# Turning the first unit of a feed-forward network in 32x32 blocks on VectorE, moving the blocks by DMA, and running that unit second

## The chip, the cores and the metric

The kernel runs on one core of a Trainium2 chip. The metric is the device time of one execution in microseconds (us): 575.26 us is the median of three runs of the kernel before (575.2 to 575.7). A lower time is better.

## What is computed

A decoder trunk of two layers over 256 tokens of 1024 features, all in float32: layer 0 mixes tokens with a gated short convolution, layer 1 with causal attention over eight heads that reads K and V projected once after layer 0. Each layer ends in the same feed-forward network, and the change is about the beginning of that network:

```python
def conv_ffn(h, w_up, w_conv, b_conv, w_down):     # h: 256 x 1024, F = 2816
    g, u = jnp.split(h @ w_up, 2, axis=-1)
    g = causal_dwconv(g, w_conv) + b_conv          # three taps along the tokens
    return (jax.nn.silu(g) * u) @ w_down

x = x + conv_ffn(rmsnorm(x, norm_ffn[i]), ffn_w_up[i], ffn_conv[i], ffn_conv_b[i], ffn_w_down[i])
```

## The kernel before, in words

**Weights.** All weights are cut into 106 slots of 128 x 2048 float32 (1 MB). SyncE (SP) loads them in order into a ring of six raw buffers (`load`, line 341); the load of slot s waits until slot s-6 has been split. ScalarE (ACT) writes the high part of a slot (`hi`, line 427), VectorE (DVE) the rest (`lo`, line 775), and TensorE (PE) multiplies high by high, high by low and low by high. Each engine works through a queue of its own, in the order in which the code is written, and the engines wait for each other on semaphores (`slot_done`, `f_cross`, `f_sum`, `tap0`, `conv_op`, `silu_done`, `act_full`, `act_hi_ready`, `act_lo_ready` and others).

**A network.** There are 22 pairs of 128 gate and up features, in 11 units of 256 features: a gate slot, an up slot and, for the unit two places earlier, a down slot. F stands below for the first slot of a network (`FFN[l]`, l = 0 and 1), so F and F+1 are gate and up of unit 0, F+2 and F+3 those of unit 1, F+4 and F+5 those of unit 2, F+6 is the down slot of unit 0, F+7 and F+8 are gate and up of unit 3, F+9 is the down slot of unit 1, and so on. From unit 1 on, a slot (`wide_slot`, `project`, lines 1215 and 1223) leaves features on partitions and tokens along the row in PSUM bank pair 0 (gate) or 1 (up). ACT copies the cross terms out (line 537 or 544), DVE adds the main term (914, 918), ACT applies the first tap and the bias (`tap_zero`, 515), DVE the two other taps (`taps`, 893), ACT the silu (523), DVE multiplies by the up half (`glued`, 900), ACT writes the high part of the product (`acts`, 527) and DVE the low part (905). `down` (lines 1278 to 1282) multiplies the product by the down slot. A bank pair is free for the next unit when DVE has read it (`f_sum`).

**The opening.** Unit 0 comes right behind the norm, when the normed activations become ready 128 tokens at a time. `open_two` (`rows_of_two`, lines 1265 and 1270) therefore makes it with tokens on partitions: tokens 0 to 127 into bank `by_rows[0]` (it signals `rows_done`), tokens 128 to 255 into `by_rows[1]` (`slot_done`), each 128 x 512. ACT copies each of them to SBUF (`copy_opening`, 509), and TensorE transposes each with four 128x128 transposes into banks `acc00` and `acc01` (`turn_opening`, 1359): the four for the first tokens stand ahead of slot F+2, the four for the others between its two halves (`two_after_opening`). Unit 0 then goes through taps, silu, product and split on ACT and DVE ahead of unit 1. The order on PE behind the opening is: slot F+2, F+3, F+4, F+5, down slot F+6 (`down(l, 2)`, waits for the low part of unit 0's product), F+7, F+8, F+9, and so on. The order of ACT and DVE is that of `ffn(l)` in their blocks. Both networks are built by the same functions.

Of the kernel before, what the change touches and what calls it, by code (L numbers as in the profile page):

```python
# [28 lines left out]
P = 128  # L29
EPS = 1e-6  # L30
RAW = 6
# [29 lines left out]
def build(nc, x, x_columns, weights, params, norm_ffn, final_norm, out, F, TAPS):  # L61
# [52 lines left out]
    assert place(V0 - 2) == place(V0 + 2) == place(V0 + 6) and place(V0 - 1) == place(V0 + 3) == place(V0 + 5)  # L114

    def gate_slot(l, j):
        return FFN[l] + (2 * j if j < 2 else 3 * j - 2)
# [8 lines left out]
    with ExitStack() as ctx:  # L126
        def sb(name, shape, dt=F32):
            return ctx.enter_context(nc.sbuf_tensor(name, shape, dt))
# [23 lines left out]
        ident = sb("ident", [P, P])  # L152
        warm_tile = sb("warm_tile", [P, P])
        par = sb("par", [P, TAPS * KD + 2 * ((TAPS + 1) * FT + KD)])
        inv_ms = sb("inv_ms", [P, 2])
# [20 lines left out]
        logits = scratch[:, 0:768].rearrange("p (e n) -> p e n", e=2)  # L176
        opening = scratch[:, 1024:2048].rearrange("p (t n) -> p t n", t=2)
        whole = scratch[:, 1024:2048].rearrange("p (b e n) -> p b e n", b=2, e=2)
# [41 lines left out]
        late_normed = sem("late_normed")  # L220
        opening_copied = sem("opening_copied")
        opening_T = sem("opening_T")
        first_landed = [sem(f"first_landed{q}") for q in range(3)]
# [110 lines left out]
        def _(sp):  # L334
# [34 lines left out]
            load_half(3, 0, fourth_landed)  # L369
            load_half(3, 1, landed[3])  # L370
            for s in range(4, SLOTS):
                load(s)
            for h in range(2):
# [47 lines left out]
        def _(act):  # L421
# [80 lines left out]

            def copy_opening(s, t, o, r):

                if t:
                    act.wait_ge(slot_done, s + 2)
                else:
                    act.wait_ge(rows_done, r)
                act.activation(opening[:, t, :], by_rows[t], ACT.Copy).then_inc(opening_copied, 1)

            def tap_zero(l, j, gate, turn=None):
# [17 lines left out]
            def unit(l, j, turn=None):  # L529

                s, U = gate_slot(l, j), l * UNITS + j
                if j >= 3:
                    hi(s + 2, turn)
                act.wait_ge(slot_done, after(s + 1, turn, TURN))
                if U:
                    act.wait_ge(conv_op, after(4 * U, turn, 4 * LOOPED))
                act.activation(whole[:, 0], cross[0], ACT.Copy).then_inc(f_cross, 1)  # L537
                hi(s + 3, turn)
                act.wait_ge(f_sum, after(f_turn(l, j, 0), turn, 2 * LOOPED))
                tap_zero(l, j, whole[:, 0], turn)  # L540
                silu(U, j, turn)
                act.wait_ge(slot_done, after(s + 2, turn, TURN))
                act.wait_ge(act_full, after(U, turn, LOOPED))
                act.activation(whole[:, 1], cross[1], ACT.Copy).then_inc(f_cross, 1)  # L544
                hi(s + 4, turn)
                acts(U, j, turn)

            def ffn(l):
                s, U = FFN[l], l * UNITS
                copy_opening(s, 0, l, 1 if l == 0 else 4)  # L550
                hi(s + 3)
                copy_opening(s, 1, l, None)
                hi(s + 4)
                act.wait_ge(opening_T, 2 * l + 1)
                tap_zero(l, 0, acc[0][0][:].rearrange("p (e n) -> p e n", e=2))
                silu(U, 0)
                acts(U, 0)
                unit(l, 1)
                unit(l, 2)
                with act.Fori(0, TURNS) as turn:  # L560
                    for j in range(3, 3 + LOOPED):
                        unit(l, j, turn)
                if l == 0:
                    hi_ahead(1)
                    hi(V0)
# [204 lines left out]
        def _(dve):  # L770
# [113 lines left out]
            def taps(l, j, gate, turn=None):  # L884
                U, g = l * UNITS + j, glu[:, j % 2]
                dve.wait_ge(tap0, after(U + 1, turn, LOOPED))
                for back in (1, 2):
                    for e in range(2):
                        if back == 2:
                            dve.wait_ge(conv_op, after(4 * U + e + 1, turn, 4 * LOOPED))  # L890
                        f = after(2 * j + e, turn, 2 * LOOPED)
                        dst = g[:, e, back:S]
                        dve.scalar_tensor_tensor(out=dst, in0=gate[:, e, 0:S - back],  # L893
                                                 scalar=f_par[:, l, bass.ds(f + (TAPS - 1 - back) * FT, 1)],
                                                 in1=dst, op0=ALU.mult, op1=ALU.add).then_inc(conv_op, 1)

            def glued(l, j, up, turn=None):
                U, g = l * UNITS + j, glu[:, j % 2]
                dve.wait_ge(silu_done, after(U + 1, turn, LOOPED))
                dve.tensor_tensor(g, g, up, ALU.mult).then_inc(act_full, 1)  # L900

            def acts(l, j, turn=None):
                U, g = l * UNITS + j, glu[:, j % 2]
                dve.wait_ge(act_hi_ready, after(U + 1, turn, LOOPED))
# [3 lines left out]
            def unit(l, j, turn=None):  # L908
# [13 lines left out]
                acts(l, j, turn)  # L922

            def ffn(l):
                s = FFN[l]
                lo(s + 2)
                lo(s + 3)
                lo(s + 4)
                taps(l, 0, acc[0][0][:].rearrange("p (e n) -> p e n", e=2))
                dve.wait_ge(opening_T, 2 * l + 2)  # L930
                glued(l, 0, acc[0][1][:].rearrange("p (e n) -> p e n", e=2))
                acts(l, 0)
                unit(l, 1)
                unit(l, 2)
                with dve.Fori(0, TURNS) as turn:
# [248 lines left out]
        def _(pe):  # L1184
# [168 lines left out]

            def turn_opening(o, t):

                pe.wait_ge(opening_copied, 2 * o + t + 1)
                for b in range(2):
                    for e in range(2):
                        last = pe.transpose(acc[0][b][:, 256 * e + P * t:256 * e + P * t + P],
                                            opening[:, t, 256 * b + P * e:256 * b + P * e + P], ident[:])  # L1360
                    if t:
                        last.then_inc(opening_T, 1)

            def two_after_opening(s, o):

                wait_slot(s)
                turn_opening(o, 0)
                project(s, 0, hA, (0,))
                turn_opening(o, 1)
                project(s, 0, hA, (1,)).then_inc(slot_done, 1)  # L1370
                wide_slot(s + 1, 1, hA)

# [26 lines left out]
            def down(l, j, turn=None):  # L1399

                U = l * UNITS + j - 2
                pe.wait_ge(act_lo_ready, after(U + 1, turn, LOOPED))
# [210 lines left out]
```

## Time and profile before

| | |
|---|---|
| median of 3 runs | 575.26 us |
| the profiled execution | 575.42 us |
| its span, from the first to the last instruction | 573.6 us |
| granted TensorE clock, mean share of full speed | 0.998 |
| busy: PE, weight loads of PE, DVE, ACT, POOL | 99%, 85%, 73%, 56%, 4% |
| DMA: share of the span on 16 engines | 52% |

The views used below are: the page's busy shares; the waits of one engine (what it sat idle for, in total, how often, longest); the chain of work that ended last, in order of time; the timeline of one engine (start, duration, line, operation, count, and in brackets the idle time before it); the groups of instructions by line and shape; and the list of DMA issues with the time to landing. In the chain a matmul counts from the end of the one before it to its own end; in the timeline it counts from its own start, and as matmuls are pipelined one of 512 columns lasts 0.39 us there while the next starts 0.23 us behind it.

### The profile page before, as it was taken

The page shows a single profiled execution, that of the slowest core. Times are in us where ns is not written, and L with a number is a line of the kernel's source. Part 1 is how long each engine was busy: PE and PEld are TensorE (multiplying, and loading weights), DVE is VectorE, ACT ScalarE, POOL GpSimd, SP SyncE. Part 2 cuts the span into 40 slices and gives each one's busy share as a digit, 9 for nine tenths or more (in the row PEclk, how much of TensorE's full clock was granted, in tenths as well). Part 3 has the DMA queues.
Part 4 walks back from the last instruction along what each step waited for, and adds up shares of the span by engine and source line. Part 5 has one row for each costly group of instructions (what it writes and reads, how often), then busy time and mean ns, then how long its engine had stood idle before and what let it go on. Part 6 is the DMA issues. An engine that isn't in the chain of part 4 may idle for free.

```text
span 573.6 us, 7862 instructions
## 1 busy us (share of the span) xinstructions
PE 566.0 (99%) x3036; PEld 489.7 (85%) x3036; DVE 418.2 (73%) x514; ACT 321.8 (56%) x415; POOL 21.6 (4%) x26
## 2 busy tenths in 40 slices
PE   8999999999999999999999999999999999999996
PEld 7888988898888888888888899888988888888885
DVE  4799987678666666676886688896786666666764
ACT  6844554565655455457456766745656554554543
POOL 0114001000000000000000000210000000000001
PEclk9999999999999999999999999999999999999999
DMA  8986656446555556555544443364355555564001
GB/s 281 419 334 231 237 193 256 184 146 212 178 198 221 180 187 219 163 191 164 216 163 177 175 149 146 117 250 185 147 202 183 201 221 175 192 220 147 1 2 73
DMA packets 17314, 108.08 MB, mean 188 GB/s; under 512 B 1920, under 2 KB 2176, under 8 KB 5248
## 3 DMA queue, kind: packets, MB, share of 16 engines
q1 hardware_dynamic: 16128, 104.78, 50.0%
q10 hardware_dynamic: 1152, 2.82, 1.4%
q8 instruction: 24, 0.39, 0.3%
q14 instruction: 10, 0.08, 0.0%
HBM read 106.55 MB, written 1.05 MB: 188 GB/s over the span
## 4 chain that ended last, share of the span: by engine, by line
PE 94%; DVE 2%; DMA 1%; issue 1%; POOL 0%; ACT 0%; SPq 0%; POOLq 0%; DVEq 0%
PE pair L1215 35%; PE pair L1223 18%; PE acc L1278 8%; PE acc L1280 8%; PE acc L1282 8%; PE pair L1265 5%; PE pair L1270 3%; PE pair L1240 1%; DMA raw<-in_weights 1%; PE acc L1190 1%; PE acc L1189 1%; PE acc L1188 1%; PE pair L1292 1%; PE pair L1249 1%; DVE wgt L775 1%
## 5 line engine op out<-in xcount | busy, mean ns | idle before, releaser
L775 DVE TENSOR_TENSOR wgt<-raw,wgt 128x2048 fp32r<-128x2048 f32 x90 | 206.2, 2297 | 56.6 <-ACT wgt L427 56.3
L1215 PE MATMUL pair<-hA,wgt 128*128 128x512 f32 x832 | 197.9, 391 | 0.0
L427 ACT ACTIVATE wgt<-raw 128x2048 fp32r<-128x2048 f32 x91 | 173.7, 1911 | 22.3 <-PE acc L1282 21.7
L1215 PEld LDWEIGHTS pair<-hA,wgt 128*128 128x128 f32 x832 | 154.1, 188 | 30.7
L1223 PEld LDWEIGHTS pair<-hA,wgt 128*128 128x128 f32 x832 | 103.8, 191 | 3.0 <-DVE gain L944 0.6
L1223 PE MATMUL pair<-hA,wgt 128*128 128x256 f32 x832 | 104.8, 283 | 0.4 <-DVE gain L944 0.4
L1278 PE MATMUL acc<-wgt,kq_hi 128*128 128x512 f32 x156 | 48.0, 389 | 0.0
L1282 PE MATMUL acc<-wgt,kq_lo 128*128 128x512 f32 x156 | 48.0, 389 | 0.0
L1280 PE MATMUL acc<-wgt,kq_hi 128*128 128x512 f32 x156 | 48.0, 389 | 0.0
L523 ACT ACTIVATE begin<-begin 128x512 f32<-128x512 f32 x22 | 13.9, 633 | 59.7 <-DVE begin L893 59.7
L537 ACT ACTIVATE begin<-pair 128x512 f32<-128x512 f32 x20 | 11.9, 594 | 58.3 <-PE pair L1223 58.3
L914 DVE TENSOR_TENSOR begin<-begin,pair 128x512 f32<-128x512 f32 x20 | 13.7, 686 | 30.9 <-ACT begin L537 30.9
L1278 PEld LDWEIGHTS acc<-wgt,kq_hi 128*128 128x128 f32 x156 | 29.3, 188 | 6.1
L1280 PEld LDWEIGHTS acc<-wgt,kq_hi 128*128 128x128 f32 x156 | 29.3, 188 | 6.1
L1282 PEld LDWEIGHTS acc<-wgt,kq_lo 128*128 128x128 f32 x156 | 29.3, 188 | 6.1
L893 DVE SCALAR_TENSOR_TENSOR begin<-begin,par 128x255 f32<-128x255 f32 (+1 forms) x80 | 33.2, 477 | 0.0
L1265 PE MATMUL pair<-wgt,hA 128*128 128x512 f32 x128 | 32.6, 393 | 0.0
L918 DVE TENSOR_TENSOR begin<-begin,pair 128x512 f32<-128x512 f32 x20 | 13.8, 688 | 23.7 <-ACT begin L544 23.7
L1265 PEld LDWEIGHTS pair<-wgt,hA 128*128 128x128 f32 x128 | 23.7, 188 | 5.1 <-issue 0.3
L386 POOL TENSOR_TENSOR rstd<-msq,minus_half 128x1 f32<-128x1 f32 x10 | 7.6, 758 | 421.1 <-DVE msq L807 417.4
L515 ACT ACTIVATE begin<-begin,par 128x256 f32<-128x256 f32 x40 | 21.6, 589 | 1.5 <-DVE begin L914 1.5
L444 ACT ACTIVATE acc<-xs 128x512 f32<-128x512 f32 x19 | 11.3, 597 | 19.8 <-DVE xs L796 15.4
(181 smaller groups left out, 614.5 us busy)
## 6 DMA issues: line engine op xcount, KB each, us to landing
raw<-in_weights SPq DMA_DIRECT2D x94, 1024.0 KB, 4.8
raw<-in_weights SPq DMA_DIRECT2D x8, 256.0 KB, 8.4
raw<-in_weights SPq DMA_DIRECT2D x4, 512.0 KB, 11.0
xs<-in_x SPq DMA_DIRECT2D x2, 512.0 KB, 10.3
gain<-in_norm_ffn ACTq DMA_DIRECT2D x2, 512.0 KB, 3.6
begin<-in_x_columns ACTq DMA_DIRECT2D x3, 256.0 KB, 7.7
gain<-in_final_norm ACTq DMA_DIRECT2D x1, 512.0 KB, 5.2
out<-begin SPq DMA_DIRECT2D x2, 256.0 KB, 2.0
```

The costliest lines, as they stand in the source:

```text
L427: act.activation(split_slot(s)[0], raw[:, s % RAW, :], ACT.Copy).then_inc(w_hi_ready, 2 if s + 1 in AHEAD else 1)
L515: ins = act.activation(g[:, e, :], gate[:, e, :], ACT.Identity, bias=f_par[:, l, bass.ds(f + TAPS * FT, 1)], scale=f_par[:, l, bass.ds(f + ...
L523: act.activation(g, g, ACT.Silu).then_inc(silu_done, 1)
L775: dve.tensor_tensor(wlo, raw[:, s % RAW, :], whi.bitcast(F32), ALU.subtract).then_inc(w_lo_ready, 2 if s + 1 in AHEAD else 1)
L893: dve.scalar_tensor_tensor(out=dst, in0=gate[:, e, 0:S - back], scalar=f_par[:, l, bass.ds(f + (TAPS - 1 - back) * FT, 1)], in1=dst, op0=A ...
L1215: last = pe.matmul(pair[b][:, e, :].rearrange("p (a n) -> p a n", a=2), whi[:, w], hid[:, :, k, :], start=first and k == 0, stop=not first ...
L1223: last = pe.matmul(pair[b][:, e, 0:S], wlo[:, w], hid[:, 0, k, :], start=first and k == 0, stop=k == KD - 1)
L1265: pe.matmul(dst, hA[:, 0, k, tok], wgt[:, part, a:b + 1:b - a, w], start=k == 0 and part == 0, stop=False)
L1270: last = pe.matmul(dst, hA[:, 1, k, tok], wgt[:, 0, a:b + 1:b - a, w], start=False, stop=k == KD - 1)
L1278: pe.matmul(acc[t][h][:], ah, wh[h], start=first, stop=False)
L1280: pe.matmul(acc[t][h][:], ah, wl[h], start=False, stop=False)
L1282: last = pe.matmul(acc[t][h][:], al, wh[h], start=False, stop=h == closes)
```

## The change

- The eight transposes of each opening on TensorE and ACT's two copies to SBUF are gone. In their place DVE transposes each `by_rows` bank from PSUM to SBUF in one instruction of 32x32 blocks (`turn_opening` on DVE; it writes into `v_own`, which is idle then), and SP issues 16 DMAs for each 128 tokens (`move_opening`) that carry pieces of 32 partitions x 512 bytes from `v_own` to `kq_first` (also idle then). The 16 DMAs for tokens 0 to 127 stand ahead of the load of slot F+8 in SP's queue, those for tokens 128 to 255 ahead of that of F+9.
- PE runs slots F+2 and F+3 as ordinary slots, each behind a wait for one of the two VectorE transposes (they read the banks that the slots overwrite).
- On ACT and DVE unit 1 now comes first and unit 0 second (`opened_unit`), then unit 2. The semaphore counts follow (`unit_count`). PE's order of slots is as before.
- In `opened_unit` ACT first waits for the 32 DMAs and copies the gate half into `v_own` (two copies of 128 x 256), applies the first tap from there, and DVE makes the product in two halves of 128 x 256.
- ACT's table load for silu is called forth by a tiny silu of 2 columns ahead of unit 1.

```diff
--- before.py
+++ after.py
@@ -112,6 +112,10 @@
 
     assert place(V0 + 4) == place(V0) == 2
     assert place(V0 - 2) == place(V0 + 2) == place(V0 + 6) and place(V0 - 1) == place(V0 + 3) == place(V0 + 5)
+
+    def unit_count(l, j):
+
+        return l * UNITS + (1 - j if j < 2 else j)
 
     def gate_slot(l, j):
         return FFN[l] + (2 * j if j < 2 else 3 * j - 2)
@@ -151,6 +155,7 @@
         dist = sb("dist", [P, 384])
         ident = sb("ident", [P, P])
         warm_tile = sb("warm_tile", [P, P])
+        silu_warm = sb("silu_warm", [P, 2])
         par = sb("par", [P, TAPS * KD + 2 * ((TAPS + 1) * FT + KD)])
         inv_ms = sb("inv_ms", [P, 2])
         sumsq = sb("sumsq", [P, 2, 2])
@@ -174,7 +179,9 @@
         conv_out = scratch.rearrange("p (f n) -> p f n", f=KD)
         glu = scratch[:, 0:1024].rearrange("p (b e n) -> p b e n", b=2, e=2)
         logits = scratch[:, 0:768].rearrange("p (e n) -> p e n", e=2)
-        opening = scratch[:, 1024:2048].rearrange("p (t n) -> p t n", t=2)
+        open_blocks = v_own[:].rearrange("p (t m n) -> p t m n", t=2, m=4)
+        opened = kq_first[:].rearrange("p a b c n -> p (a b c n)").rearrange("p (t g e n) -> p (t g) e n", t=2, g=4, e=4)
+        open_gate = v_own[:, 0:512].rearrange("p (e n) -> p e n", e=2)
         whole = scratch[:, 1024:2048].rearrange("p (b e n) -> p b e n", b=2, e=2)
         a_whole = gain[:].rearrange("p (b e n) -> p b e n", b=2, e=2)
         act_hi = kq_hi[:].rearrange("p a b n -> p (a b n)").rearrange("p (u e n) -> p u e n", u=4, e=2)
@@ -218,8 +225,10 @@
         x_T = sem("x_T")
         kv_scaled = sem("kv_scaled")
         late_normed = sem("late_normed")
-        opening_copied = sem("opening_copied")
-        opening_T = sem("opening_T")
+        opening_turned = sem("opening_turned")
+        opening_moved = sem("opening_moved")
+        open_gate_ready = sem("open_gate_ready")
+        open_full = sem("open_full")
         first_landed = [sem(f"first_landed{q}") for q in range(3)]
         second_landed = [sem(f"second_landed{q}") for q in range(3)]
         third_landed = sem("third_landed")
@@ -368,7 +377,19 @@
             sp.dma_start(par[:], params).then_inc(par_in, 16)
             load_half(3, 0, fourth_landed)
             load_half(3, 1, landed[3])
+            def move_opening(l, t):
+
+                sp.wait_ge(opening_turned, 2 * l + t + 1)
+                for g in range(4):
+                    for m in range(4):
+                        sp.dma_start(opened[32 * m:32 * m + 32, 4 * t + g, :, :],
+                                     open_blocks[32 * g:32 * g + 32, t, m, :].rearrange("p (e n) -> p e n", e=4)).then_inc(opening_moved, 16)
+
             for s in range(4, SLOTS):
+                for l in range(2):
+                    for t in range(2):
+                        if s == FFN[l] + RAW + 2 + t:
+                            move_opening(l, t)
                 load(s)
             for h in range(2):
                 sp.wait_ge(normed_ready, hidden(5, 0, h))
@@ -500,14 +521,6 @@
                 for h in range(2):
                     h_hi(2, 1, h)
 
-            def copy_opening(s, t, o, r):
-
-                if t:
-                    act.wait_ge(slot_done, s + 2)
-                else:
-                    act.wait_ge(rows_done, r)
-                act.activation(opening[:, t, :], by_rows[t], ACT.Copy).then_inc(opening_copied, 1)
-
             def tap_zero(l, j, gate, turn=None):
                 g = glu[:, j % 2]
                 for e in range(2):
@@ -528,7 +541,7 @@
 
             def unit(l, j, turn=None):
 
-                s, U = gate_slot(l, j), l * UNITS + j
+                s, U = gate_slot(l, j), unit_count(l, j)
                 if j >= 3:
                     hi(s + 2, turn)
                 act.wait_ge(slot_done, after(s + 1, turn, TURN))
@@ -540,22 +553,29 @@
                 tap_zero(l, j, whole[:, 0], turn)
                 silu(U, j, turn)
                 act.wait_ge(slot_done, after(s + 2, turn, TURN))
-                act.wait_ge(act_full, after(U, turn, LOOPED))
+                if U:
+                    act.wait_ge(act_full, after(U, turn, LOOPED))
                 act.activation(whole[:, 1], cross[1], ACT.Copy).then_inc(f_cross, 1)
                 hi(s + 4, turn)
                 acts(U, j, turn)
 
-            def ffn(l):
-                s, U = FFN[l], l * UNITS
-                copy_opening(s, 0, l, 1 if l == 0 else 4)
-                hi(s + 3)
-                copy_opening(s, 1, l, None)
-                hi(s + 4)
-                act.wait_ge(opening_T, 2 * l + 1)
-                tap_zero(l, 0, acc[0][0][:].rearrange("p (e n) -> p e n", e=2))
+            def opened_unit(l):
+                U = unit_count(l, 0)
+                act.wait_ge(opening_moved, 16 * 32 * (l + 1))
+                for e in range(2):
+                    act.activation(open_gate[:, e, :].rearrange("p (g n) -> p g n", n=32), opened[:, :, e, :], ACT.Copy).then_inc(open_gate_ready, 1)
+                act.wait_ge(open_gate_ready, 2 * l + 2)
+                tap_zero(l, 0, open_gate)
                 silu(U, 0)
                 acts(U, 0)
+
+            def ffn(l):
+                s = FFN[l]
+                hi(s + 3)
+                hi(s + 4)
+                act.activation(silu_warm[:], warm_tile[:, 0:2], ACT.Silu).then_inc(table_loaded, 1)
                 unit(l, 1)
+                opened_unit(l)
                 unit(l, 2)
                 with act.Fori(0, TURNS) as turn:
                     for j in range(3, 3 + LOOPED):
@@ -882,7 +902,7 @@
                     h_lo(n, 1)
 
             def taps(l, j, gate, turn=None):
-                U, g = l * UNITS + j, glu[:, j % 2]
+                U, g = unit_count(l, j), glu[:, j % 2]
                 dve.wait_ge(tap0, after(U + 1, turn, LOOPED))
                 for back in (1, 2):
                     for e in range(2):
@@ -895,12 +915,12 @@
                                                  in1=dst, op0=ALU.mult, op1=ALU.add).then_inc(conv_op, 1)
 
             def glued(l, j, up, turn=None):
-                U, g = l * UNITS + j, glu[:, j % 2]
+                U, g = unit_count(l, j), glu[:, j % 2]
                 dve.wait_ge(silu_done, after(U + 1, turn, LOOPED))
                 dve.tensor_tensor(g, g, up, ALU.mult).then_inc(act_full, 1)
 
             def acts(l, j, turn=None):
-                U, g = l * UNITS + j, glu[:, j % 2]
+                U, g = unit_count(l, j), glu[:, j % 2]
                 dve.wait_ge(act_hi_ready, after(U + 1, turn, LOOPED))
                 dve.tensor_tensor(act_lo[:, j % 4], g, act_hi[:, j % 4].bitcast(F32),
                                   ALU.subtract).then_inc(act_lo_ready, 1)
@@ -921,16 +941,28 @@
                 lo(s + 4, turn)
                 acts(l, j, turn)
 
+            def turn_opening(l, t):
+                dve.wait_ge(*((slot_done, FFN[l] + 2) if t else (rows_done, 4 if l else 1)))
+                dve.transpose(open_blocks[:, t].rearrange("p m (e n) -> p m e n", e=4),
+                              by_rows[t].rearrange("p (e m n) -> p m e n", e=4, m=4)).then_inc(opening_turned, 1)
+
+            def opened_unit(l):
+                U, g = unit_count(l, 0), glu[:, 0].rearrange("p e (g n) -> p e g n", n=32)
+                taps(l, 0, open_gate)
+                dve.wait_ge(silu_done, U + 1)
+                for e in range(2):
+                    dve.tensor_tensor(g[:, e], g[:, e], opened[:, :, 2 + e, :], ALU.mult).then_inc(open_full if e == 0 else act_full, 1)
+                acts(l, 0)
+
             def ffn(l):
                 s = FFN[l]
+                turn_opening(l, 0)
                 lo(s + 2)
+                turn_opening(l, 1)
                 lo(s + 3)
                 lo(s + 4)
-                taps(l, 0, acc[0][0][:].rearrange("p (e n) -> p e n", e=2))
-                dve.wait_ge(opening_T, 2 * l + 2)
-                glued(l, 0, acc[0][1][:].rearrange("p (e n) -> p e n", e=2))
-                acts(l, 0)
                 unit(l, 1)
+                opened_unit(l)
                 unit(l, 2)
                 with dve.Fori(0, TURNS) as turn:
                     for j in range(3, 3 + LOOPED):
@@ -1351,24 +1383,11 @@
                 rows_of_two(s, 0, n, lambda: transposes(n, 1)).then_inc(rows_done, 1)
                 rows_of_two(s, 1, n).then_inc(slot_done, 2)
 
-            def turn_opening(o, t):
-
-                pe.wait_ge(opening_copied, 2 * o + t + 1)
+            def two_after_opening(s, l):
+
                 for b in range(2):
-                    for e in range(2):
-                        last = pe.transpose(acc[0][b][:, 256 * e + P * t:256 * e + P * t + P],
-                                            opening[:, t, 256 * b + P * e:256 * b + P * e + P], ident[:])
-                    if t:
-                        last.then_inc(opening_T, 1)
-
-            def two_after_opening(s, o):
-
-                wait_slot(s)
-                turn_opening(o, 0)
-                project(s, 0, hA, (0,))
-                turn_opening(o, 1)
-                project(s, 0, hA, (1,)).then_inc(slot_done, 1)
-                wide_slot(s + 1, 1, hA)
+                    pe.wait_ge(opening_turned, 2 * l + b + 1)
+                    wide_slot(s + b, b, hA)
 
             def wide_slot(s, b, hid, turn=None):
                 if b:
@@ -1398,7 +1417,7 @@
 
             def down(l, j, turn=None):
 
-                U = l * UNITS + j - 2
+                U = unit_count(l, j - 2)
                 pe.wait_ge(act_lo_ready, after(U + 1, turn, LOOPED))
                 deep_slot(gate_slot(l, j) + 2, act_pair(j - 2), first=(j == 2), turn=turn, closes=1 if l and j == UNITS - 1 else None)
 
```

## Rows read from the trace of the kernel before

**Rows 1.** The page: busy time, share of the span, instructions.

```profile
PE 566.0 (99%) x3036; PEld 489.7 (85%) x3036; DVE 418.2 (73%) x514; ACT 321.8 (56%) x415; POOL 21.6 (4%) x26
```

**Rows 2.** Waits of PE, longest in total first: us, times, longest.

```profile
PE pair L1427 <- DVE warm_tile L1039: 1.1, 1, 1.1
```

**Rows 3.** The chain, first opening: start, us, what.

```profile
108.49 0.91 PE pair L1270 x4
109.40 0.44 PE acc L1359 x4
...
112.63 0.44 PE acc L1359 x4
...
117.78 7.28 PE pair L1215 x32
...
132.55 0.45 PE acc L1278 x2
...
137.99 3.63 PE pair L1215 x16
```

**Rows 4.** The chain where K is projected behind V by rows.

```profile
305.07 3.63 PE pair L1215 x16
...
312.53 7.28 PE pair L1215 x32
```

**Rows 5.** The chain, second opening.

```profile
396.43 0.44 PE acc L1359 x4
...
404.82 7.28 PE pair L1215 x32
```

**Rows 6.** Timeline, 299 to 311 us, ACT: first reading of a bank behind such a slot.

```profile
310.65 0.60 ACT L580 ACTIVATE begin<-pair 128x512 f32<-128x512 f32 x1 [1.34 <-PE pair L1223]
```

**Rows 7.** Timeline of ACT, first network.

```profile
109.93 1.91 ACT L427 ACTIVATE wgt<-raw 128x2048 fp32r<-128x2048 f32 x1
...
113.93 1.28 ACT L523 ACT_TABLE_LOAD   x1
...
120.03 1.08 ACT L515 ACTIVATE begin<-begin,par 128x256 f32<-128x256 f32 x2
...
143.66 0.60 ACT L537 ACTIVATE begin<-pair 128x512 f32<-128x512 f32 x1 [3.71 <-PE pair L1223]
```

**Rows 8.** Timeline of DVE, first network.

```profile
104.00 4.72 DVE L775 TENSOR_TENSOR wgt<-raw,wgt 128x2048 fp32r<-128x2048 f32 x2
...
132.64 1.66 DVE L893 SCALAR_TENSOR_TENSOR begin<-begin,par 128x255 f32<-128x255 f32 x4
...
139.49 0.69 DVE L905 TENSOR_TENSOR kq_lo<-begin,kq_hi 128x512 fp32r<-128x512 f32 x1
...
148.30 1.66 DVE L893 SCALAR_TENSOR_TENSOR begin<-begin,par 128x255 f32<-128x255 f32 x4
```

**Rows 9.** Groups by line and shape, DVE and ACT: busy us, mean ns, idle before.

```profile
L994 DVE TENSOR_TENSOR v_lo<-pair,v_hi 128x512 fp32r<-128x512 f32 x2 | 1.4, 687 | 1.3 <-ACT v_hi L594 1.3
L1117 DVE TENSOR_TENSOR mix_lo<-acc,mix_hi 128x256 fp32r<-128x256 f32 x6 | 2.3, 419 | 0.2 <-ACT mix_hi L715 0.2
```

```profile
L523 ACT ACTIVATE begin<-begin 128x512 f32<-128x512 f32 x22 | 13.9, 633 | 59.7 <-DVE begin L893 59.7
L527 ACT ACTIVATE kq_hi<-begin 128x512 fp32r<-128x512 f32 x22 | 13.6, 616 | 1.6 <-DVE begin L900 1.6
L584 ACT ACTIVATE kq_first<-begin 128x256 f32<-128x256 f32 x8 | 3.3, 409 | 3.0 <-DVE begin L983 3.0
```

**Rows 10.** Timeline of SP: DMA issues back to back, and one alone.

```profile
0.74 4.99 SPq L352 DMA_DIRECT2D raw<-in_weights  x8
...
8.96 0.91 SPq L346 DMA_DIRECT2D raw<-in_weights  x2
9.91 0.91 SPq L341 DMA_DIRECT2D raw<-in_weights  x2
```

```profile
106.31 0.33 SPq L341 DMA_DIRECT2D raw<-in_weights  x1
```

**Rows 11.** DMA issues: count, KB each, median us from issue to landing.

```profile
raw<-in_weights SPq DMA_DIRECT2D x94, 1024.0 KB, 4.8
...
out<-begin SPq DMA_DIRECT2D x2, 256.0 KB, 2.0
```

**Rows 12.** Timeline of PE at the start of down slot F+6.

```profile
132.16 0.41 PEld L1278 LDWEIGHTS acc<-wgt,kq_hi 128*128 128x128 f32 x2
132.39 0.62 PE L1278 MATMUL acc<-wgt,kq_hi 128*128 128x512 f32 x2
```

## The prediction

> **What bounds the kernel now.** I read three views in this order. The busy shares put PE at 99% of the span [rows 1]. The waits of PE say that this is no average over unlike stages: its longest wait is 1.1 us at the very start [rows 2], and none lies in either network. The chain agrees: through both openings it runs on PE alone, group after group without a gap [rows 3, 5]. So a microsecond taken from PE's queue is a microsecond of the kernel, as long as ACT, DVE and the DMAs still deliver in time; a microsecond of theirs counts only from the point where PE waits for it.
>
> **What goes from PE.** Behind `rows_of_two` the chain passes to the transposes at 108.49 + 0.91 = 109.40 and reaches the second half of slot F+3 at 117.78: 8.38 us for one slot, eight transposes and the first half of the next slot [rows 3]. The same without transposes stands where K is projected behind V: from 305.07 to 312.53, 7.46 us [rows 4]. The difference, 0.92 us, is the price of the eight transposes (two groups of 0.44 and a little at each seam). The second opening takes 396.43 to 404.82, 8.39 us [rows 5], the same. Two openings give 1.84 us. Everything on PE behind F+3 comes 0.92 us earlier: the down slot F+6 is due at 132.55 - 0.92 = 131.63 instead of 132.55 [rows 3].
>
> The Trainium skill (VectorE: DVE Perf Modes, The three transpose paths) gives a 128x128 transpose on TensorE 390 ns in bf16; 16 of them would be 6.2 us, and an estimate by that page 569.0 us. The trace has 0.44 us for four in a row, since they are pipelined, so the sum does without the page. The same page's rules for kernel authors would have TensorE do a 128x128 transpose when the result may go to PSUM; that rule looks at one transpose and not at which engine is full.
>
> **What comes in, one by one** (times of the first network; the second has the same distances).
>
> *The turns on DVE.* No 32x32 transpose stands in the trace. The nearest row is DVE reading a 128x512 bank, 0.69 us [rows 9]; a split of 128x2048 (half of 4.72, 2.36 us [rows 8]) is the other bound, four times the elements. I take 0.69 since the size and the bank are the same. The first turn follows `rows_done` at about 104.00, where DVE now starts its two splits [rows 8], and ends at 104.69; lo(F+2) then ends at about 107. The second waits for the second bank at 109.40, ends at 110.1, and lo(F+3) ends at 112.3, lo(F+4) at 114.5. This is a new wait: behind it in DVE's queue stands lo(F+3), which used to be done by 108.72 (104.00 + 4.72 [rows 8]). Who waits for it is PE at slot F+3, due at 109.40 + 5.54 = 114.94 (a gate slot alone: 3.63, and half of the remaining 3.83 of the 7.46 [rows 4]). Cover 2.3 us. DVE is wanted next at 115.6, when ACT's first copy of unit 1 is made (114.98, below, and 0.60). So a turn may take up to about 2.7 us before it costs anything: nothing.
>
> A page-only price: by the skill's same table (311 ns on VectorE for 128x128 in bf16) a turn would be an estimated 1.24 us, still under that cover.
>
> *ACT.* Two copies fall away. hi(F+4) starts at 109.44 rather than 109.93 [rows 7]; the table load (1.28 us [rows 7]) and a tiny silu then end near 112.8, ahead of slot F+2's end: nothing.
>
> *The chain that is now late.* Unit 0 stands behind unit 1 on ACT and DVE, but PE still wants it first, for F+6 at 131.63. Before, it was the first thing that both engines did.
> - Slot F+2 behind the rows: the first ACT reading comes 5.58 us after the rows' end (310.65 - 305.07 [rows 4, 6]): 114.98.
> - From that reading to the taps: 143.66 to 148.30, 4.64 us [rows 7, 8]: 119.62.
> - From the taps to the end of the unit's low part: 132.64 to 139.49 + 0.69, 7.54 us [rows 8]: 127.16. Unit 1 is done, and the taps of unit 0 can start at 127.08.
> - Unit 0: taps 1.66, silu 0.63, two products of 0.42 of which the second starts 0.33 behind (0.75), high part 0.62, low part 0.69 [rows 8, 9], with about 0.03 at each of four handovers: 4.47. It ends at 131.55.
>
> PE starts the first weight load of a down slot 0.39 us before the slot's place in the chain (132.16 against 132.55 [rows 3, 12]), so it wants the signal at 131.24. It comes 0.31 late, with the handover about 0.35 us. That is my value for the new stall of PE per opening: 0.70 us for both. The chain has some 25 links, and 0.02 us on each moves it by 0.5, so I put its bounds at 0 and 0.9 us per opening.
>
> *Further behind.* ACT takes up unit 2 only behind unit 0's high part, at 130.7. Its copy (0.5 to the next instruction) and hi(F+7) (1.9) end at 133.1, lo(F+7) (2.3) at 135.4, the taps at 137.1, silu and the next copy at 138.1, hi(F+8) at 140.0 and lo(F+8) at 142.3. PE needs lo(F+8) at the start of that slot (narrow half first), 137.99 - 0.92 + 0.35 + 5.54 = 142.96, its weight load 0.3 earlier. Cover 0.3 us: nothing, but thin. From unit 3 on ACT's idle time of 3.71 us before the gate copy [rows 7] absorbs the rest.
>
> *The moves.* SP issues 32 DMAs. Bounds for one issue: 0.33 us alone, 0.475 in a row (8.96 to 9.91 for two), 0.62 for the eight at the start (4.99 / 8) [rows 10]. I take 0.475, a row of plain back-to-back issues. From the first turn at 104.7: 16 moves, the load of F+8, 16 moves, 33 x 0.475 = 15.7 us, last issue over at 120.4. Landing: 2.0 us for a 256 KB store, 4.8 for a whole slot [rows 11]; pieces of 16 KB are nearer to the first, and F+8's load, issued at 112.3, is through by 117.1. So 122.4. ACT gets there at 124.66, and its copies (2 x 0.41, overlapped) and first tap (1.08 [rows 7, 9]) end at 126.5, while DVE has time until 127.05. The moves are needed by 125.2. Cover 2.8 us: nothing; without it every microsecond counts fully, twice.
>
> *SP's queue.* The loads of F+8 and F+9 are issued at 112.3 and 120.4 instead of 106.31 [rows 10] and 108.7, and each takes 4.8 us [rows 11]. The high part of F+8 is begun at 138.1, that of F+9 behind it. Nothing. The moves carry 512 KB per opening, half a slot's bytes.
>
> **The sum.** 575.42 us was the profiled execution (span 573.6 and 1.8 around it), the median 575.26, 0.16 less. 575.26 - 1.84 + 0.70 = 574.12 us.
>
> **The rivals.**
> *No stall* (0.25). Unit 0 is done 0.3 us earlier than I have it, for instance as a handover is shorter. Then the whole 1.84 comes through: 573.4 us. For it speaks that my chain misses by only 0.35 us in 22; against it that every link was taken from a row of the same instruction.
> *The moves land late* (0.18), the case on the other side. Place: ACT's wait in `opened_unit`. Price: each us past 125.2, at both openings. It decides from a pitch of (125.2 - 2.0 - 104.7) / 33 = 0.56 us per issue. At the 0.62 of the first eight loads they land at 127.2, 2.0 us late: 574.12 + 2 x 2.0 = 578.1 us. It is slower than before by over 0.2% from a pitch of 0.60. For it: those eight loads got slower one after another. Against it: each of them had 128 rows, the moves have 32, and ACT was issuing beside them.
> *Longer on ACT and DVE* (0.08). The thin cover at lo(F+8) fails too, or a turn takes over 2.7 us: a stall of 1.0 to 1.5 us per opening, 575.4 to 576.4 us.
> *The change does not do what it says* (0.04): the compiler cuts a move into 128-byte pieces or puts in waits; somewhere above 577 us.
>
> By the Trainium skill (DMA: Bandwidth & Descriptors, Anatomy of one DMA) a DMA has a fixed cost of some 2.0 us, of which most is the receipt of completion. Were it paid one after another, 32 would take 65 us and both networks would stand still. The eight loads issued within 5 us [rows 10] show that issue doesn't wait for completion, so I give that no chance of its own.
>
> **How the numbers follow.** My forecast, a stall of 0.1 to 0.9 us per opening, has 0.45 (its own range 573.6 to 575.2). 0.2% is 1.15 us, about what a measurement of this kernel can tell from no change; faster means under 574.11. The forecast lies on that line, so half of its chance goes to either side. Faster: 0.25 + 0.22 = 0.47. Slower (over 576.41): 0.18 and a little of the last two, 0.21. Same: 0.32. The range runs from 573.2 (all of the gain, and 0.2 of spread) to 577.0, which holds moves late by up to 1.4 us.
>
> **What would show it.** Right: no L1359 on PE; the chain from the rows' end to the second half of F+3 at 7.46 us; a PE wait of 0.1 to 0.9 us at the first matmul of `down(l, 2)` on DVE's low part, twice, and no other; moves landed by 125. Wrong: PE waiting longer there, with ACT's gate copy idle for a DMA (late moves); PE waiting at the narrow half of F+3 (slow turn) or F+8; SP's issues more than 0.56 us apart.

## The result, and the profile after

| | before | changed |
|---|---|---|
| median us (range) | 575.36 (575.2 to 575.7, 4 runs) | 583.61 (582.4 to 584.5, 4 runs) |
| ratio, 95% interval | | 1.0141 (1.0129 to 1.0153) |
| profiled execution, span | 575.42, 573.6 | 584.47, 582.7 |
| mean granted clock | 0.998 | 0.990 |

The change made the kernel 8.3 us slower. The forecast was 574.1 us, the range ended at 577.0.

The waits of PE (us in total, times, longest), changed kernel. The first line is new; [rows 2] has the longest of before.

```profile
PE acc L1310 <- issue: 6.5, 2, 4.2
PE pair L1446 <- DVE warm_tile L1071: 1.1, 1, 1.1
```

L1310 is the first matmul of a down slot. Here is the chain of the changed kernel through the first opening (start, us, what):

```profile
108.63 0.91 PE pair L1302 x4
109.54 3.63 PE pair L1247 x16
113.17 3.83 PE pair L1255 x32
117.00 7.28 PE pair L1247 x32
...
128.11 3.65 PE pair L1247 x16
131.77 2.33 issue
134.09 1.19 PE acc L1310 x2
135.28 0.85 PE acc L1312 x2
136.14 0.85 PE acc L1314 x2
136.99 0.71 PE acc L1310 x2
137.70 0.45 PE acc L1312 x2
```

Three things are in it. From the end of the rows to the second half of slot F+3 it is 109.54 to 117.00, 7.46 us, where [rows 3] had 8.38: the transposes are gone and their 0.92 us is gained. Then PE stands idle for 2.33 us at F+6. And behind that wait two matmuls of 512 columns take 0.85 us, while further down, and in all of [rows 3], they take 0.45. The busy time by stretches says why (stretch, busy us and count of each engine, granted clock, DMA share, GB/s):

```profile
131.80:134.00 2.20, 0.00 (x0) 0.00 (x0) 1.46 (x4) 1.37 (x4) 0.00 (x0) 0.99 1.08 458
134.10:137.30 3.20, 3.20 (x8) 2.52 (x9) 2.21 (x2) 2.43 (x3) 0.00 (x0) 0.50 0.99 420
137.60:141.00 3.40, 3.40 (x17) 2.82 (x16) 2.22 (x6) 1.51 (x3) 0.00 (x0) 1.00 0.77 267
```

The granted clock went to 0.50, which is 1.2 instead of 2.4 GHz, when PE had done nothing for over two microseconds, and PE worked at half speed when it came back. The prediction left this out. The Trainium skill (TensorE: Matmul & The Clock Gate, HAM oscillation — how this bites in real kernels) says that a kernel whose TensorE waits too long between pieces of work starts each next piece at the low clock. These rows agree: 0.50 behind an idle time of 2.33 us. The second opening is worse:

```profile
421.93 4.18 issue
426.12 1.19 PE acc L1310 x2
427.31 0.85 PE acc L1312 x2
```

Who made PE wait stands in ACT's timeline and SP's (ACT in the first opening, SP in the first, ACT in the second):

```profile
127.59 0.72 ACT L566 ACTIVATE v_own<-kq_first 128x256 f32<-128x256 f32 x2 [2.70 <-DMA kq_first<-v_own]
```

```profile
104.88 10.82 SPq L385 DMA_DIRECT2D kq_first<-v_own  x16
115.75 0.58 SPq L350 DMA_DIRECT2D raw<-in_weights  x1
116.38 10.00 SPq L385 DMA_DIRECT2D kq_first<-v_own  x16
```

```profile
419.62 0.72 ACT L566 ACTIVATE v_own<-kq_first 128x256 f32<-128x256 f32 x2 [4.56 <-DMA kq_first<-v_own]
```

ACT stands ready for the blocks at 124.9 and gets them at 127.6. SP issues without a pause from 104.9 to 126.4: 16 moves take 10.00 to 10.82 us. They are 0.633 us apart, where I had put 0.475, but for one move in the first 16 whose issue took 1.33 us by itself. The VectorE turns are cheap: one of them is

```profile
104.14 0.71 DVE L946 STREAM_TRANSPOSE v_own<-pair 128x512 f32<-128x512 f32 x1
```

### The profile page after: what moved, and what is told of

It reads as the page before. It is cut to its first block, busy times and chain, and to the rows that moved or that the text cites. A ratio compares the mean times of both kernels' runs of the same rounds, so it can differ in the third digit from the quotient of the medians.

```text
span 582.7 us, 7898 instructions
## 1 busy us (share of the span) xinstructions
PE 568.4 (98%) x3020; PEld 490.7 (84%) x3020; DVE 421.3 (72%) x520; ACT 321.4 (55%) x417; POOL 21.6 (4%) x26
## 4 chain that ended last, share of the span: by engine, by line
PE 93%; issue 2%; DVE 2%; DMA 1%; POOL 0%; ACT 0%; SPq 0%; POOLq 0%; DVEq 0%
PE pair L1247 34%; PE pair L1255 18%; PE acc L1310 8%; PE acc L1312 8%; PE acc L1314 8%; PE pair L1297 5%; PE pair L1302 3%; PE pair L1272 1%; DMA raw<-in_weights 1%; PE acc L1222 1%; PE acc L1220 1%; PE acc L1221 1%; PE pair L1324 1%; PE pair L1281 1%; DVE wgt L795 1%
## 5 line engine op out<-in xcount | busy, mean ns | idle before, releaser
L1310 PE MATMUL acc<-wgt,kq_hi 128*128 128x512 f32 x156 | 49.9, 402 | 6.5 <-issue 6.5
L1312 PE MATMUL acc<-wgt,kq_hi 128*128 128x512 f32 x156 | 49.3, 398 | 0.0
L536 ACT ACTIVATE begin<-begin 128x512 f32<-128x512 f32 x22 | 13.9, 632 | 62.6 <-DVE begin L913 62.6
L1310 PEld LDWEIGHTS acc<-wgt,kq_hi 128*128 128x128 f32 x156 | 30.1, 195 | 13.5 <-issue 7.3
L1312 PEld LDWEIGHTS acc<-wgt,kq_hi 128*128 128x128 f32 x156 | 30.2, 194 | 6.5
```

The source lines that it names most:

```text
L536: act.activation(g, g, ACT.Silu).then_inc(silu_done, 1)
L1310: pe.matmul(acc[t][h][:], ah, wh[h], start=first, stop=False)
L1312: pe.matmul(acc[t][h][:], ah, wl[h], start=False, stop=False)
```

## The experiments

Theory A: the serial issue of the moves makes them late, and everything else of the change does what the sum said. Rival B: the swapped order of the units is itself too long for ACT and DVE. C and the others stand with their runs. All ratios are against the kernel before on the same chip (575.3 to 575.4 us).

### Leave the moves out (e1)

```diff
-            def move_opening(l, t): ...            # SP's 32 DMAs
-        open_blocks = v_own[:]...
+        open_blocks = kq_first[:]...               # the turn writes where unit 0 is read
-                act.wait_ge(opening_moved, 16 * 32 * (l + 1))
+                act.wait_ge(opening_turned, 2 * (l + 1))
```

> The 32 DMAs of each opening are left out: VectorE turns the blocks straight into the buffer that unit 0 is read from, and ScalarE waits for the turns alone, so the blocks stand in the wrong places and the output is not the reference's. Everything else is as in the changed kernel. Theory A (the moves land late; the order of the units costs only a short wait): the low part of unit 0 is ready about 131.6 us into the span, TensorE waits 0.2 to 0.5 us at each down slot F+6, the granted clock stays at full speed, and the time is 573.6 to 574.7 us. Theory B (the swap of the units itself makes the chain on ScalarE and VectorE too long): TensorE still waits 2 us or more at F+6 and the time stays above 578 us.

The blocks stay where the turn put them, so this kernel computes something else; its times are what is read. 574.15 us, ratio 0.9979 (0.9970 to 0.9988). PE is idle for only 0.07 us at F+6, and the low part of unit 0 ends near where the chain of the prediction had it (131.55), in DVE's timeline:

```profile
130.65 0.69 DVE L912 TENSOR_TENSOR kq_lo<-begin,kq_hi 128x512 fp32r<-128x512 f32 x1 [0.70 <-ACT kq_hi L527]
```

130.65 + 0.69 = 131.34. The rows end at 109.15 in this run, 0.25 us earlier than before, so the distance from there is 22.19 us against 22.15 in the prediction. All of the loss hangs on the moves; the swap and the turns are not it. B falls.

### Sixteen moves instead of 32 (e2)

```diff
-                sp.wait_ge(opening_turned, 2 * l + t + 1)
+                sp.wait_ge(opening_turned, 2 * l + 2)
...
-                        sp.dma_start(opened[32 * m:32 * m + 32, 4 * t + g, :, :],
-                                     open_blocks[32 * g:32 * g + 32, t, m, :]...).then_inc(opening_moved, 16)
+                        sp.dma_start(opened[32 * m:32 * m + 32, g::4, :, :]...,
+                                     open_blocks[32 * g:32 * g + 32, :, m, :]).then_inc(opening_moved, 16)
```

> Sixteen moves for each opening instead of 32: each carries the pieces of both halves of the tokens (32 partitions, two pieces of 512 bytes), all behind the second turn. Theory A, if an issue costs the 0.63 us of the changed kernel whatever it carries: 16 issues end at 110.3 + 10.1 = 120.4 us, the last lands at about 122.3, before ScalarE gets there at 124.8, and the time is 573.6 to 574.7 us, that of the run without moves. Rival C (the issue costs by the piece: 64 pieces take twice 0.63 us): the issues end at 130.6, as late as before or later, and the time is 583 us or more.

574.40 us, ratio 0.9985 (0.9976 to 0.9994): with its output whole, the changed design is a little faster than before. SP's timeline:

```profile
110.20 10.60 SPq L385 DMA_DIRECT2D kq_first<-v_own  x16
```

Twice the bytes and twice the pieces cost the same: 0.64 us per issue in the steady part. It is the count of DMAs that is paid. C falls. The chain shows the short wait that the prediction had put at 0.35 us:

```profile
131.64 0.07 issue
131.71 0.69 PE acc L1309 x2
132.40 0.47 PE acc L1311 x2
...
137.43 0.68 PE pair L1246 x3
```

0.07 idle and 0.69 instead of 0.45 for the first pair, and full clock behind it. From the end of the slot before (131.64) to the slot behind the down slot (137.43) it is 5.79 us, where [rows 3] has 5.44 (132.55 to 137.99): a stall of 0.35 us.

### The order of the units alone (e3)

```diff
 # kernel before, TensorE transposes kept
+                unit(l, 1)
                 act.wait_ge(opening_T, 2 * l + 1)
                 tap_zero(l, 0, acc[0][0][:].rearrange("p (e n) -> p e n", e=2))
...
-                unit(l, 1)
```

This is ACT's part; DVE's order is swapped in the same way, and the tiny silu ahead of unit 1 is in.

> The kernel before with one part of the change: the TensorE transposes stay, no VectorE turns and no moves, but unit 1 goes ahead of unit 0 on ScalarE and VectorE. Theory A: the chain behind slot F+2 and TensorE's arrival at F+6 are both 0.92 us later than in the changed kernel, so the wait is the same 0.2 to 0.5 us per opening and the time is 575.8 to 576.4 us against 575.4 before. Theory B: waits of 2 us and more, above 580 us.

576.11 us, ratio 1.0015 (1.0006 to 1.0024): 0.8 us for both openings by the medians, where the sum had 0.70. The chain has, in the first opening,

```profile
132.71 0.05 issue
...
138.48 1.59 PE pair L1222 x7
```

138.48 - 132.71 = 5.77 us against 5.44 before: 0.33 us. So the swap costs, and a kernel that takes only the swap is slower.

### Fill the wait on VectorE (e4)

```diff
 # on top of e2
                 glued(l, j, whole[:, 1], turn)
                 lo(s + 4, turn)
-                acts(l, j, turn)
+                if j > 1:
+                    acts(l, j, turn)
...
                 taps(l, 0, open_gate)
+                acts(l, 1)                          # low part of unit 1, while ACT makes unit 0's silu
                 dve.wait_ge(silu_done, U + 1)
```

> Sixteen moves as above, and the low part of unit 1 on VectorE goes behind the taps of unit 0, into the time in which VectorE waits for unit 0's silu. Theory A: the taps of unit 0 start 0.5 to 0.6 us earlier, the wait at F+6 disappears, and the time is 573.3 to 573.9 us, all of the 1.84 us of the transposes. If instead the short wait at F+6 has another cause than VectorE's queue, the time equals that of the run with 16 moves.

573.51 us, ratio 0.9970 (0.9958 to 0.9981), the fastest of all. The chain has no idle time and no longer first pair any more:

```profile
127.62 3.65 PE pair L1248 x16
131.28 0.45 PE acc L1311 x2
...
136.72 1.36 PE pair L1248 x6
```

136.72 - 131.28 = 5.44 us, the same as in [rows 3]. 575.32 - 573.51 = 1.81 us, against 1.84 for sixteen transposes in the sum.

### What an issue costs (e5)

```diff
                 for g in range(4):
+                    if l == 0:
+                        sp.dma_start(opened[:, 4 * t + g, :, :]..., open_blocks[:, t, g, :])   # 128 partitions, SBUF to SBUF
+                        continue
                     for m in range(4):
-                        sp.dma_start(opened[32 * m:32 * m + 32, ...], open_blocks[32 * g:32 * g + 32, t, m, :]...)
+                        sp.dma_start(opened[32 * m:32 * m + 32, ...], weights[0, 32 * g:32 * g + 32, 128 * m:128 * m + 128])
```

> A look at what an issue costs on SyncE. First opening: the 16 moves of each half are replaced by 4 of 128 partitions x 512 bytes within SBUF. Second opening: 16 moves per half of 32 partitions x 512 bytes as before, but from HBM (a weight slot) instead of from SBUF. Unit 0 then works on wrong blocks, so the output is not the reference's. In the changed kernel one move is issued every 0.63 us, whole-slot loads from HBM in a row every 0.475 us. Theory D (a source in SBUF makes the issue dear): 0.63 us apart in the first opening, 0.475 in the second. Theory E (few partitions make it dear): 0.475 in the first, 0.63 in the second. Theory F (neither; it is the form of a small DMA in a row): 0.63 in both.

SP's timeline, first opening and then twelve issues of the second:

```profile
104.77 2.54 SPq L385 DMA_DIRECT2D kq_first<-v_own  x4
107.35 0.59 SPq L350 DMA_DIRECT2D raw<-in_weights  x1
```

```profile
393.99 5.53 SPq L389 DMA_DIRECT2D kq_first<-in_weights  x12
```

Four DMAs of 128 partitions within SBUF are (107.35 - 104.77) / 4 = 0.645 us apart; twelve of 32 partitions from HBM are 0.464 apart (5.53 us to the end of the twelfth, which took 0.42 itself). Not the number of partitions and not the size: in these rows a DMA from SBUF to SBUF costs SyncE more than one from HBM to SBUF (theory D). A source in SBUF alone does not do it where a DMA stands by itself. The changed kernel's first store of the output, from SBUF to HBM, was issued in 0.35 us, and its first moves, behind a pause of SP too, in 0.59 and 0.51:

```profile
575.49 0.35 SPq L396 DMA_DIRECT2D out<-begin  x1
395.05 0.51 SPq L385 DMA_DIRECT2D kq_first<-v_own  x1
```

That points to both ends in SBUF. Stores in a row, which would settle it, stand in no run. With 32 moves in the second opening at 0.464 us PE had no wait beyond the 0.07 us of e2 there, nor with the eight of the first, and the single run took 574.41 us: at the pitch that I had assumed the forecast comes out.

### How lateness is paid (e6, e7)

```diff
 # e2, with n - 16 further moves of 32 KB ahead of the real ones (n = 22 in e6, 28 in e7)
+                for k in range(n - 16):
+                    q = 32 * (k % 4)
+                    sp.dma_start(spare[q:q + 32, k // 4, :, :], open_blocks[q:q + 32, :, k // 4, :]).then_inc(opening_moved, 16)
```

> The run with 16 moves per opening, with 6 more of the same size ahead of them into a spare buffer, for which ScalarE waits too. Theory A: an issue is 0.64 us, so 22 end at 110.2 + 14.1 + 0.4 = 124.7 us, landed at 126.2, some 0.9 us behind the point (125.3) from which lateness counts. TensorE waits 1.1 to 1.5 us at each F+6 and the time is 574.4 + 1.8 = 576.2 us if the granted clock holds. If the clock falls behind a wait of this length as it did behind the changed kernel's 2.3 us (half speed for 3.4 us, 1.7 us lost), another 0.5 to 2 us: up to 578.2.

575.20 us, ratio 0.9998 (0.9988 to 1.0007). A miss by 1 us to the good side: the blocks came at 126.06 in the first opening, 1.2 us behind ACT, and 0.7 behind it in the second, where no issue was a slow one (the 22 starts span 13.4 us there, 13.9 in the first). PE was idle for 0.85 and 0.35 us, where 1.1 to 1.5 was expected, and the clock held (first opening):

```profile
131.80:132.50 0.70, 0.00 (x0) 0.00 (x0) 0.70 (x2) 0.70 (x2) 0.00 (x0) 1.00 1.11 468
132.70:137.00 4.30, 4.30 (x20) 3.51 (x21) 3.30 (x4) 2.31 (x3) 0.00 (x0) 1.00 0.94 394
```

> As with 22, with 12 more moves. Theory A: 28 issues end at 110.2 + 17.9 + 0.4 = 128.5, landed at 130.0, 4.7 us late; waits of 5.0 us per opening, 574.4 + 9.4 = 583.8 us from the waits alone. The granted clock: in the changed kernel a wait of 2.3 us was followed by 3.4 us at half speed and one of 4.2 us by 6.8 us. If the loss grows with the wait like that, another 3.5 to 4 us per opening: 591 us. If the clock falls for a fixed time, 587 us; if it was not the wait that brought it down, 584 us.

587.85 us, ratio 1.0223 (1.0198 to 1.0248). PE waits 9.9 us in total (5.1 at most), and in the first opening:

```profile
131.80:136.60 4.80, 0.00 (x0) 0.00 (x0) 3.18 (x8) 2.24 (x5) 0.00 (x0) 0.75 1.02 430
136.70:141.00 4.30, 4.30 (x10) 3.38 (x11) 3.31 (x4) 2.38 (x3) 0.00 (x0) 0.50 0.94 396
```

```profile
131.58 5.06 issue
136.64 1.19 PE acc L1314 x2
...
144.38 1.81 PE pair L1251 x8
```

The wait itself was as expected. The price of the clock was left open among three values, and the time came out near the 587 of a fixed fall and not at the 591 of a loss that grows with the wait. The down slot takes 144.38 - 136.64 = 7.74 us instead of 5.44, so 2.3 us are lost behind the wait of 5.1 us, where the changed kernel loses 1.8 behind 2.3 us and 2.55 behind 4.2. Part of the slow time lies in the wait, where it costs nothing (the clock's mean was already 0.75 over the idle stretch).

### GpSimd issues half of the moves (e8)

```diff
 # SP keeps move_opening(l, 0); in GpSimd's block, behind the roots of the norm
+                if z in (1, 3):
+                    pool.wait_ge(opening_turned, 2 * l + 2)
+                    for g in range(4):
+                        for m in range(4):
+                            pool.dma_start(opened[32 * m:32 * m + 32, 4 + g, :, :],
+                                           open_blocks[32 * g:32 * g + 32, 1, m, :]...).then_inc(opening_moved_1, 16)
```

> The changed kernel with the 16 moves of tokens 128 to 255 issued by GpSimd, which is idle there, instead of by SyncE. Theory A (the serial issue on one queue is what made the moves late): SyncE's 16 end at 115.7 us as before, GpSimd's run beside them from 110.3 on. No GpSimd DMA stands in a trace yet: at up to 0.83 us each they land by 125.3 and the time is 573.9 to 574.9 us; at 1.2 us each they land at 131, later than now, and the time is 587 us or more. Rival (the DMA engines or their rings, not the issue, are the limit): the moves land no earlier than 127.5 us whoever issues them, and the time stays at 583 us.

574.51 us, ratio 0.9986 (0.9977 to 0.9996). The timelines of POOL and SP:

```profile
110.11 8.05 POOL L445 DMA_DIRECT2D kq_first<-v_own  x16 [10.03 <-DVE v_own L954]
```

```profile
104.40 10.44 SPq L386 DMA_DIRECT2D kq_first<-v_own  x16
```

All 32 moves were issued by 118.2 instead of 126.4. The engines that carry them were not the limit, which the DMA share of the changed kernel during the issues says too (forty slices of 104 to 116 us, most of them 0 to 3 tenths):

```profile
DMA  5799742202020201030010002020101011010202
```

## Why the prediction was wrong, step by step

- *What bounds the kernel, and what the transposes cost: right.* PE's chain rules; 0.92 us per opening went, and 1.81 of 1.84 us came through once nothing else stood in the way (e4).
- *The turns on DVE: right.* 0.71 us against 0.69, hidden. Only the cover was read too wide: a turn of 2.7 us would not have been free, since DVE had 1.07 us to spare ahead of unit 1's first addition (the prediction's own 115.6 - 114.5), and what comes behind that is the chain that is late anyway:

```profile
115.75 0.69 DVE L934 TENSOR_TENSOR begin<-begin,pair 128x512 f32<-128x512 f32 x1 [1.07 <-ACT begin L550]
```

- *The late chain and its stall: right in place and size.* Unit 0's low part 22.15 us behind the rows by the sum, 22.19 in e1. The stall of 0.35 us per opening is 0.35 in e2's first, and e3 has 0.33. A miss of 0.02 us in a chain of some 25 links is better than its rows can promise, so part of it is luck.
- *Cover at lo(F+8), SP's later loads: right.* No further wait of PE in the networks stands in any run.
- *The moves: the term that failed.* I chose 0.475 us per issue from loads out of HBM as "plain back-to-back issues"; from SBUF to SBUF it is 0.633 to 0.645 (changed kernel, e2, e5). The difference of 0.158 us times 33 is 5.2 us, and the cover was 2.8. The bound of 0.62, from loads of another kind, was nearly right, and I gave the case 0.18. That the landing then comes out as measured (104.7 + 33 x 0.633 + 2.0 = 127.6) is luck in part. A move landed 1.8 us from the start of its issue, where the sum has 2.0 from the end of the last one's turn, 0.8 more, and the one issue of 1.33 us took 0.7 that the sum did not have. The 1.8 us are not far from the fixed cost of 2.0 that the prediction has from the Trainium skill, out of a section on DMAs that GpSimd issues. The nearest row was nearest by how the DMAs follow each other, but differed in where they read; nothing in the trace of before read from SBUF into SBUF, which was a reason to price the case by the far bound.
- *The price of the late case: too low.* The rival at 0.62 us had 578.1 us; its 2.0 us of lateness is what the first opening shows (2.33 us idle, against the 0.35 that were there anyway). Missing were two things. The clock: the first down slot of the changed kernel takes from 134.09 to 141.33, 7.24 us, where [rows 3] has 132.55 to 137.99, 5.44; 1.80 us lost, and by the same reckoning 2.55 in the second opening (426.12 to 434.11). And 1.85 us more idle time in the second opening (4.18 against 2.33). 578.1 + 4.35 + 1.85 = 584.3, close to the 584.47 of the profiled execution, the longest of the four (median 583.61).
- *Where the 1.85 us come from* was not tested. In the second opening 15 of the last move's 16 completions had come by 417.56 and the last one at 419.60, and from 417.11 to 418.57 a 16 KB packet of the instruction queue was under way. The trace does not say on which of the 16 DMA engines. The list of DMA issues from 416 to 420 us has both:

```profile
q8 instruction: 1, 0.02, 2.3%
...
kq_first<-v_own SPq DMA_DIRECT2D x1, 16.0 KB, 3.8
```

That it was the code load which held the move back is argued, not shown. A single issue of 1.3 us stands in each opening too (at 109.31 and 396.87, among others of 0.59), near such a packet (at 109.37 and 396.64).

## What to carry to other kernels

Price a chain of small DMAs by count times the issue time of a DMA of the same kind (which queue, which ends), and where no such row exists take the far bound; here 16 DMAs instead of 32, or the second half on another queue, turned 8.3 us of loss into 0.9 us of gain. When work that TensorE is to wait for has a cover of only two or three microseconds, a miss can cost more than itself: 0.85 us of idle time left the clock alone, 2.33 us were followed by 1.8 us of lost speed. Moving a unit behind another one is not free where its consumer comes soon: look for an instruction of the same engine that can go into its waits (e4).

## What I had not expected of the hardware

- SyncE issued a DMA within SBUF every 0.633 to 0.645 us, with 32 or 128 partitions, one or two pieces of 512 bytes; one from HBM every 0.464 to 0.475 us. GpSimd issued the same moves within SBUF 0.49 us apart (110.11 to 118.16 for 16).
- Waits of PE of 0.07, 0.35 and 0.85 us left the granted clock at full speed; behind waits of 2.3, 4.2, 4.9 and 5.1 us it stood at half speed, and came back only when PE had worked again for several microseconds (until 137.4 in the changed kernel's first opening, PE being back at work since 134.09). What each cost in lost speed was 1.8, 2.55, 2.45 and 2.3 us in the same order, so no more behind the longest wait than behind that of 4.2 us.
